# Experts' rows moved by exact lists, and a token's two rows stored side by side

## The reference

```python
def hier_moe(h, ...):            # h (T, 1024); T = 768 in layer 0, 512 in layer 1
    group_p = softmax(h @ group_w + group_b)        # 4 groups, the best one
    g_top, g_sel = top_k(group_p, 1)
    within = expert logits of that group            # 8 experts, the best two
    top_p, top_i = top_k(softmax(within), 2)
    weights = g_top * top_p / sum(top_p)            # two per token
    for each of the 32 experts e, on the rows x of its tokens:
        y = (silu(x @ w_gate[e]) * (x @ w_up[e])) @ w_down[e]   # 1024 -> 512 -> 1024
    return sum over a token's two experts of weight * y
```

## Time and profile before

| | |
|---|---|
| median of 3 runs | 2139.3 us (2135.72 to 2140.68) |
| the profiled execution | 2136.48 us, its span 2134.8 us |
| PE busy | 1700.6 us, 80% of the span |
| DVE, ACT, POOL busy | 689.1, 445.5, 241.1 us |
| DMA | 565.49 MB, mean 265 GB/s |
| mean granted clock of PE | 0.912 |

### The profile page before, as it was taken

One profiled execution on the slowest core, in us unless ns is written; L12 is line 12 of the kernel. 1 busy time (PEld: TensorE's weight loads), 2 busy tenths in 40 slices (PEclk: granted clock), 3 DMA queues, 4 the chain that ended last, 5 costly groups with the idle time before them and its releaser, 6 DMA issues. The chain is left out here.

```text
span 2134.8 us, 25794 instructions
## 1 busy us (share of the span) xinstructions
PE 1700.6 (80%) x9072; PEld 889.9 (42%) x9073; DVE 689.1 (32%) x1259; ACT 445.5 (21%) x816; POOL 241.1 (11%) x342
## 2 busy tenths in 40 slices
PE   5999999798598789998627899999947799856551
PEld 3444444645344334444315446555523344433330
DVE  2405574733311111112133347775331111111114
ACT  3103333101001111111134125553101111111102
POOL 1002520311101000001020200000111000000001
PEclk9999999898699999999867999999959899988885
DMA  9785844301999999999962002001089999999993
GB/s 366 264 272 199 286 143 151 135 30 54 369 377 381 413 413 420 422 410 397 422 262 85 2 1 89 1 1 33 40 342 384 414 421 407 403 410 415 413 409 141
DMA packets 98356, 565.49 MB, mean 265 GB/s; under 512 B 15924, under 2 KB 34192, under 8 KB 58728
## 3 DMA queue, kind: packets, MB, share of 16 engines
q1 hardware_dynamic: 85248, 522.46, 62.0%
q0 software_dynamic: 7744, 26.22, 3.5%
q10 hardware_dynamic: 5288, 15.80, 1.9%
HBM read 522.95 MB, written 41.50 MB: 264 GB/s over the span
## 5 line engine op out<-in xcount | busy, mean ns | idle before, releaser
L2069 PE MATMUL exp_gps<-moew_wg,all_hT 128*64 128x512 f32 (+1 forms) x480 | 241.3, 627 | 34.1 <-DMA moew_wu<-in_moe_w_up 31.8
L2063 PE MATMUL exp_gps<-moew_wg,all_hT 128*32 128x256 f32 x1088 | 158.0, 455 | 103.4 <-DMA moew_wu<-in_moe_w_up 98.2
L2070 PE MATMUL exp_ups<-moew_wu,all_hT 128*64 128x512 f32 (+1 forms) x480 | 239.6, 624 | 0.0
L587 PE MATMUL abp_ps<-ab_w,all_hT 128*128 128x512 f32 x384 | 169.6, 597 | 0.6 <-PE abp_ps L591 0.3
L2063 PE MATMUL exp_ups<-moew_wu,all_hT 128*32 128x256 f32 x1088 | 158.4, 455 | 0.8 <-issue 0.8
L2063 PEld LDWEIGHTS exp_gps<-moew_wg,all_hT 128*32 128x32 f32 x1088 | 77.7, 130 | 180.9 <-issue 138.0
L2069 PEld LDWEIGHTS exp_gps<-moew_wg,all_hT 128*64 128x64 f32 (+1 forms) x480 | 78.3, 167 | 169.7 <-issue 169.7
L2097 PE MATMUL exp_yps<-moew_wd,all_hT 128*64 128x512 f32 (+1 forms) x240 | 116.5, 602 | 20.4 <-issue 20.4
L2194 DVE TENSOR_TENSOR all_hT<-all_hT,exp_ups 64x512 f32<-64x512 f32 (+1 forms) x30 | 20.7, 690 | 344.3 <-ACT all_hT L2141 344.3
L2099 PE MATMUL exp_yps<-moew_wd,all_hT 128*64 128x512 f32 (+1 forms) x240 | 116.0, 600 | 0.0
L587 PEld LDWEIGHTS abp_ps<-ab_w,all_hT 128*128 128x128 f32 x384 | 71.6, 190 | 98.5 <-issue 96.8
(11 more groups left out here) (417 smaller groups left out, 2532.6 us busy)
## 6 DMA issues: line engine op xcount, KB each, us to landing
moew_wg<-in_moe_w_gate SPq DMA_DIRECT2D x64, 2048.0 KB
moew_wu<-in_moe_w_up SPq DMA_DIRECT2D x64, 2048.0 KB
moew_wd<-in_moe_w_down SPq DMA_DIRECT2D x64, 2048.0 KB, 32.1
all_X<-in_ada_w SPq DMA_DIRECT2D x40, 1024.0 KB, 8.0
ab_w<-in_ab_w_in SPq DMA_DIRECT2D x6, 2048.0 KB, 9.4
ys<-abp_zero SPq DMA_DIRECT2D x32, 384.0 KB, 8.3
ys<-exp_y ACTq DMA_DIRECT2D x13, 512.0 KB
ab_rows<-in_ada_w SPq DMA_DIRECT2D x6, 1024.0 KB, 15.3
```

The source lines that it names most:

```text
L587: last = nc.tensor.matmul(ps[i % RB][:], hT[:, kk, what * P:(what + 1) * P], w[n % S][:, kk, :], start=(kk == 0), stop=(kk == KD - 1))
L2063: last = nc.tensor.matmul(bank[lo + j * Q:lo + (j + 1) * Q, 0:HC], x[:, k, 0:Q], wt[:, k, j * HC:(j + 1) * HC], start=(k == 0), stop=(k == ...
L2069: nc.tensor.matmul(gps[0:rows, :], x[:, k, 0:rows], w.g[q][:, k, :], start=(k == 0), stop=(k == KD - 1))
L2070: last = nc.tensor.matmul(ups[at:at + rows, :], x[:, k, 0:rows], w.u[q][:, k, :], start=(k == 0), stop=(k == KD - 1))
```

## The change

Four edits hang together.

- The tables. In place of the token number t, the one-hot product carries 2 t + k - 4096, k being 0 or 1 for the token's first and second expert. With 4096 added, a filled place holds 2 t + k and an empty one 4096 (`NONE`); a minimum with `limit` leaves that, but makes the last of the 128 places 1536 (`SPARE`) if it is empty. This is `r.row`, the row of `ys` that the result goes to; `r.tok` is that shifted right by one. `r.slot` is gone. `h_rows` and `ys` get one spare row at their ends; the one of `h_rows` is set to zero.
- Every gather is issued for 128 places with a bound: an index over the bound is left out. The count isn't read by Pool any more, and four gathers run ahead instead of three.
- The store goes to Pool as an indirect scatter by `r.row` with a bound, after two waits (`y_act`, `y_dve`), each followed by a small operation that marks its place. Pool waits for the landing before it goes on, and then frees `y`. Its gather for expert n + 4 comes before the scatter of expert n. Clearing of `ys` is gone; `y` in SBUF is set to zero once a layer, before routing writes its matrices there.
- The two results of token t are now rows 2 t and 2 t + 1 of `ys`, so that `load_pairs` loads a tile of 128 tokens with one plain transfer, 8 KB for each partition, issued by Pool.

```diff
@@ ab_project: clearing
-            def clear_slots(b):
-                lo = 0 if b >= E else P // 4
-                sp.dma_start(c.ys[b * P + lo:(b + 1) * P, :].rearrange("p (a n) -> p a n", a=4),
-                             zero[lo:, None, :].to_broadcast([P - lo, 4, DM // 4])).then_inc(z_stored, 16)
...
+            sp.dma_start(c.h_rows[TOK:TOK + 1, :].rearrange("p (a n) -> p a n", a=4),
+                         zero[:, None, :].to_broadcast([1, 4, DM // 4])).then_inc(z_stored, 16)
...
-                        clear_slots(n)
...
-            for b in range(len(ADA_AT), BLOCKS):
-                clear_slots(b)
-            sp.wait_ge(z_stored, 16 * BLOCKS)
+            sp.wait_ge(z_stored, 16)
@@ routing
-        index(tokid, [[P, T]], t0 * P, 1)
+        index(rowid, [[1, 2], [2 * P, T]], 2 * t0 * P - NONE, 2)
         nc.gpsimd.memset(onesE, 1.0).then_inc(io_ready, 1)
+        nc.gpsimd.memset(limit, float(NONE)).then_inc(limit_set, 1)
+        pool.wait_ge(limit_set, 1)
+        nc.gpsimd.affine_select(out=limit, in_=limit, compare_op=ALU.is_ge, fill=float(SPARE), base=P - 2,
+                                pattern=[[0, 1]], channel_multiplier=-1).then_inc(io_ready, 1)
...
+        dve.wait_ge(low_set, 1)
...
-        for k in range(2):
-            half = blk_hot[:, k * T:(k + 1) * T, :]
-            ins = V.tensor_tensor(half, half, tokid[:, :, None].to_broadcast([P, T, NB]), ALU.mult)
-            ins.then_inc(hots_done, 1) if k else link(ins)
-        link(V.scalar_tensor_tensor(out=r.slot[:, 0:2 * T], in0=blk, scalar=float(CAP), in1=row,
-                                    op0=ALU.mult, op1=ALU.add))
+        V.tensor_tensor(blk_hot, blk_hot, rowid.rearrange("p k t -> p (k t)")[:, :, None].to_broadcast([P, 2 * T, NB]),
+                        ALU.mult).then_inc(hots_done, 1)
...
-        V.tensor_copy(r.tok[:, 0:NB], lps).then_inc(listed, 1)
+        link(V.tensor_scalar(r.row[:, 0:NB], lps, float(NONE), limit[:, 0:1], ALU.add, ALU.min))
+        V.tensor_scalar(r.tok[:, 0:NB], r.row[:, 0:NB], 1, None, ALU.arith_shift_right).then_inc(listed, 1)
@@ experts: Pool
+            nc.gpsimd.memset(y_space[:], 0.0).then_inc(y_set, 1)
...
-            def turn(n, q, i):
+            def gather(n, q):
                 pool.wait_ge(xg_free, n + 1)
                 nc.gpsimd.tensor_copy(idx[q][:], r.tok[:, bass.ds(n, 1)]).then_inc(idx_done, 1)
                 pool.wait_ge(idx_done, n + 1)
                 nc.gpsimd.tensor_tensor(spare[:], spare[:], spare[:], ALU.add)
-
-                def gather(rows):
-                    nc.gpsimd.indirect_dma_start(xg[q][0:rows, :], None, c.h_rows[:, :],
-                                                 bass.IndirectOffsetOnAxis(idx[q][0:rows, :], 0)).then_inc(x_ready[q], 16)
-
-                by_rows(pool, n, gather)
-
-            turns(pool, turn)
+                nc.gpsimd.indirect_dma_start(xg[q], None, c.h_rows[:, :], bass.IndirectOffsetOnAxis(idx[q][:], 0),
+                                             bounds_check=TOK, oob_is_err=False).then_inc(x_ready[q], 16)
+
+            def scatter(n, q, i):
+                nc.gpsimd.tensor_copy(idy[q][:], r.row[:, bass.ds(n, 1)]).then_inc(idy_done, 1)
+                pool.wait_ge(idy_done, n + 1)
+                nc.gpsimd.tensor_tensor(spare[:], spare[:], spare[:], ALU.add)
+                pool.wait_ge(y_act, n + 2)
+                nc.gpsimd.tensor_tensor(mark[:, 1:2], one, one, ALU.add)
+                pool.wait_ge(y_dve, n + 2)
+                nc.gpsimd.tensor_tensor(mark[:, 2:3], one, one, ALU.add)
+                nc.gpsimd.indirect_dma_start(c.ys[:, :], bass.IndirectOffsetOnAxis(idy[q][:], 0), y[q], None,
+                                             bounds_check=SPARE, oob_is_err=False).then_inc(stored[q], 16)
+                pool.wait_ge(stored[q], i * 16 + 16)
+                nc.gpsimd.tensor_tensor(mark[:, 0:1], one, one, ALU.add).then_inc(y_free, 1)
+
+            LEAD = S + 1
+            for n in range(LEAD):
+                gather(n, n % S)
+            PAIRS = (E - LEAD) // S
+            with pool.Fori(0, PAIRS) as i:
+                for q in range(S):
+                    gather(i * S + (q + LEAD), (q + LEAD) % S)
+                    scatter(i * S + q, q, i)
...
@@ experts: ACT and DVE
-                    act.wait_ge(y_free[q], i * 16 + 16)
+                    act.wait_ge(y_free, n + 1)
...
-                    act.wait_ge(y_act, n + 2)
-                    act.wait_ge(y_dve, n + 2)
-                    act.dma_start(ys[bass.ds(n, 1), 0:rows].rearrange("o p n -> (o p) n"), y[q][0:rows, :]).then_inc(y_free[q], 16)
@@ combine and combine_into_mla
+def load_pairs(eng, c, t0, t, y_pair, x_done, got):
+
+    n = len(y_pair)
+    if t >= n:
+        eng.wait_ge(x_done, t - n + 1)
+    rows = c.ys[2 * (t0 + t) * P:2 * (t0 + t + 1) * P, :].rearrange("(p k) n -> p (k n)", k=2)
+    eng.dma_start(y_pair[t % n][:], rows).then_inc(got[t % n], 16)
...
-                for k in range(2):
-                    nc.gpsimd.indirect_dma_start(y[t % YB][k][:], None, c.ys[:, :],
-                                                 bass.IndirectOffsetOnAxis(r.slot[:, k * T + t:k * T + t + 1], 0)
-                                                 ).then_inc(got[t % YB], 16)
+                load_pairs(pool, c, 0, t, y_pair, x_done, got)
```

More of the change, by code:

```diff
@@ L357, in ab_project @@
         n4 = s.sb("n4", [P, 2 * LT])
-        zero = s.sb("zero", [P, DM // 4])
+        zero = s.sb("zero", [1, DM // 4])
         cs = s.sb("cs", [P, 2, NT - CT, RD // 2])
@@ L1633, in __init__, with routing @@
         self.gpsimd, self.tensor, self.vector, self.listed = gpsimd, tensor, vector, listed
-def routing(nc, c, layer, t0, r, s, take, take_low, banks):
+def routing(nc, c, layer, t0, r, s, take, take_low, low_set, banks):
     T = NT - t0
@@ L1657, in routing @@
     iob, iop = take("iob", [P, NB]), take("iop", [P, P])
-    tokid = take("tokid", [P, T])
+    rowid = take("rowid", [P, 2, T])
+    limit = take("limit", [P, 1])
     row_hot = take_low("row_hot", [P, 2 * T, P])
@@ L1818, in further_blocks @@
     wd_e = a["moe_w_down"][layer].rearrange("e (k p) n -> e p k n", p=P)
-    ys = c.ys.rearrange("(b p) n -> b p n", p=P)
+    one = c.ones[0:1, 0:1]
     def asked(eng):
@@ L1889, in vector @@
         with dve.If(num > 0):
-            before.stores(dve)
+            dve.sem_inc(y_done, 1)
             with dve.Fori(0, OVB) as b:
@@ L1907, with __init__ @@
 class Before:
-    def __init__(self, weights, rows, stores):
-        self.weights, self.rows, self.stores = weights, rows, stores
+    def __init__(self, weights, rows):
+        self.weights, self.rows = weights, rows
 def experts(nc, c, a, layer, t0, r, w, prefetch):
@@ L1923, in experts @@
         idx = [s.sb(f"idx{i}", [P, 1], I32) for i in range(S)]
+        idy = [s.sb(f"idy{i}", [P, 1], I32) for i in range(S)]
+        mark = s.sb("mark", [1, 3])
+        one = c.ones[0:1, 0:1]
         y_space = s.sb("y", [P, S * DM])
@@ L1955, in all_turned @@
             pool.wait_ge(xtr, E)
-        def all_stored(dve):
-            dve.wait_ge(y_free[0], 16 * (len(range(0, E, S)) + 1))
         more = further_blocks(nc, c, a, layer, t0, r, s,
-                              (w.g[0], w.u[0], w.d[0], idx[0], spare, xg[0], xT, sg, h, hT, y[0], xps, gps, ups, hps, yps),
-                              Before(all_used, all_turned, all_stored))
+                              (w.g[0], w.u[0], w.d[0], idx[0], idy[0], spare, mark, xg[0], xT, sg, h, hT, y[0], xps, gps, ups, hps, yps),
+                              Before(all_used, all_turned))
         block = s.block()
-        ys = c.ys.rearrange("(b p) n -> b p n", p=P)
-        def turns(eng, turn):
-            with eng.Fori(0, LOOPS) as i:
-                for q in range(S):
-                    turn(i * S + q, q, i)
-            for n in range(LOOPS * S, E):
-                turn(n, n % S, n // S)
-        def by_rows(eng, n, work):
-            rows = eng.value_load(r.cnt[0:1, bass.ds(n, 1)], min_val=0, max_val=TOK)
-            sized(eng, rows, work)
         def sized(eng, rows, work):
@@ L2123, in _ @@
             act.sem_inc(y_act, 1)
-            for free in y_free:
-                act.sem_inc(free, 16)
+            act.sem_inc(y_free, S)
             def x_copy(n, q):
@@ L2166, in _ @@
             more.scalar(act)
-            for q in range(S):
-                act.wait_ge(y_free[q], 16 * (len(range(q, E, S)) + 1))
         @block.vector
@@ L2232, in combine @@
         YB = 3
-        y = [[s.sb(f"y{b}{k}", [P, DM]) for k in range(2)] for b in range(YB)]
+        y_pair = [s.sb(f"y{b}", [P, 2 * DM]) for b in range(YB)]
+        y = [[pair[:, k * DM:(k + 1) * DM] for k in range(2)] for pair in y_pair]
         got = [s.sem(f"got{b}") for b in range(YB)]
@@ L2467, in routed @@
     r = Box()
-    r.slot = s.sb("slot", [P, 2 * NT], I32)
+    r.row = s.sb("row", [P, E + 2 * NT], I32)
     r.tok = s.sb("tok", [P, E + 2 * NT], I32)
```

100 lines of the change are left out of this document (49 added, 51 removed).

## The result

The changed kernel took 2152.5 us (median of 4 runs, 2150.8 to 2153.1) where the kernel before took 2139.3: ratio 1.0057, 95% interval 1.0045 to 1.0068, so 13.3 us slower. The forecast was 2165 us. Its sign was right. Its size was not, and its reason even less so: in the traces the expert stages, which were to bring +32, brought +1.9, and the two seams after them, which the sum had at +3, brought +13.6.

A forecast was written before the change was run, and what follows sets the result against it. The stream of expert weights through the 16 DMA engines was taken to bound both expert stages. 2136.5 + 32 (expert rows) - 4 (other edits) = 2164.5, given as 2165 us; own range 2145 to 2185, 8-in-10 range 2108 to 2190.

The forecast's parts named there:

- Rows of the experts: Both expert stages: skipped empty rows, but real rows crowded onto the low-place engines, lengthen the DMA stream; +32 us taken.
- the small size is cut anew over them: Gathers before the change: even a transfer of 32 rows is spread over all 16 engines; a row costs 0.187 us.
- +48: Expert stages, places in runs of four, twice: first engine carries 376 rows against 240, +136 x 0.356 = +48 us.
- the first engine has 4 rows of each of the 34 smallest experts: Expert lists of 128: fixed places in runs of four give the first engine 136 + 240 = 376 rows.
- Seams: End of each layer's expert stage: store moved to Pool, with list and landing wait, +1.5 us twice, between 0 and +3 each.
- Clearing: Projection stage: 43 clearing stores of ys, 18.4 MB, go away; between 0 and -5 us, taken as -2.
- First gather: Start of each layer's experts: Pool no longer loads a count and branches before the first gather; -1.2 us twice.
- Combine: After each expert stage: one 1 MB load for a tile replaces two gathers, one issue of 1.25 us less, twice: -2.5.
- Pool in order (rival 3): Expert stages: Pool's gather, scatter and landing wait decide once landing takes 10 us or more; +32 us more; chance 0.05.
- Equal parts (rival 1): Expert stages: real rows dealt evenly over engines, -27 us on DMA, perhaps 17 let through; 2115 us; chance 0.33.
- The sign: Whole kernel: forecast slower, 2165 us from 2136.5; chance of slower 0.57, same 0.07, faster 0.36.

## Why the prediction was wrong

- **Rows of the experts, +32 taken, +1.9 measured.** The failed step is the price in "the small size is cut anew over them". The small lists are indeed cut over all engines. (The 1344 packets named for it only showed that every transfer ends on 16 engines; the cut itself was shown later, by the list of 64.) But I priced a row of a small gather like any other, at queue 0's mean of 0.187 us, and so had the base too cheap. In fact the short gathers that the change removes were the dearest rows of all, 0.98 and 1.94 us for 32 and 64: the gathers gave -21 us, where the same step had 136 x 0.187 = +25 in its +48. The other half stands: fixed places, runs of four, "the first engine has 4 rows of each of the 34 smallest experts". On the stores' side alone that step gives 136 x 0.169 = +23 us, and the table gives +20. The row that could have warned me was queue 0 itself: 0.187 us for a gathered row against 0.169 for a stored one, a difference that I priced and did not ask about.
- **Seams, +1.5 us twice taken, +7.1 and +6.5 measured.** The step costed the list and the landing and bounded them by 0 and +3; for these alone it was right (1.7 in the second seam). It left out that an engine which is last also drains last, and that with a fresh transfer the drain takes 5.3 us. Pool's drain is in the trace of before, 64 us from the end of the stage, where it cost nothing. This term is what made the kernel slower.
- **Clearing, -2 taken, -3.3 measured** (about 4 over all traces), within its bounds of 0 and -5.
- **First gather, -1.2 us twice.** From logits to PE's first transposes 37.3 us became 36.3 in the first layer, and 34.8 became 33.8 in the second. It fits.
- **Combine, -2.5 taken.** From the first seam to the second logits it is +4.5: +1.8 in the first combine, where gates and tiles now share the queues, and +2.7 behind it from the granted clock, which the change did not make. The part after the last seam gained 0.7. One load for two gathers brought nothing that shows.
- **Pool in order (rival 3)** stated that it decides once a landing takes 10 us. (Its 11.4 us is how long PE waited for a gather, not how long the gather took to land.) A landing takes 11 to 12.4 us beside weights, Pool waits 694 us for landings in the changed kernel, and yet the stream with the wait was no longer than without: 3 us of work and the landing fit into a turn of 16 us. The threshold was too low.
- **Equal parts (rival 1)** would have asked for the long list's places to be dealt in turn. They are not.
- **The sign** was right by accident: a wrong +32 stood where a missing +11 belonged.

## What to carry to other kernels

Beside a stream of weights that fills the DMA engines, a gather into the low 32 or 64 partitions should be issued with all 128 places and the empty ones left out; a scatter from so few partitions, or a plain store, should be issued at its true length. With the old stores, or with short scatters and the last landing waited for by SP, the kernel runs in 2125.7 or 2129.4 us, 0.994 of the kernel before; these are the two to keep of this change. And whoever moves the last action of a block to another engine should look up how long that engine's drain is, and whether it was hidden so far.

## What the runs showed of the hardware

- A list of 64 rows gathered into partitions 0 to 63 uses all 16 engines at half rate (201 GB/s at a DMA share of 0.98, where full lists moved 417). Beside a stream of weights, lists of 32 and 64 rows cost it 0.98 and 1.94 us, where 128 rows cost 1.28. The same short lists in the other direction cost 0.25 to 0.31 and 0.62.
- A place left out of a list stays with its engine, as a packet of 4 bytes and 9 ns.
- Pool's drain at the end of a block took 2.7 us with its last transfer over 60 us back, 5.3 us with a store of its own landed 0.8 to 1.0 us before, and 5.7 us with one issued 0.5 us before. Begun 0.5 to 1 us after a gather's issue amid the weights it took 7.6 to 10.9 us, and ended 1.4 us after the landing in the four cases where that is on record.
